# One 512-column matmul for the high and low activations in the feed-forward and MLP input projections

## The reference

```python
def conv_gated_ffn(h, w_in, conv_w, conv_b, w_out):          # D_FF = 2816, twice
    S = h.shape[1]
    g, u = jnp.split(h @ w_in, 2, axis=-1)
    gp = jnp.pad(g, ((0, 0), (CONV_WIDTH - 1, 0), (0, 0)))
    g = conv_b + sum(conv_w[k] * gp[:, k:k + S] for k in range(CONV_WIDTH))
    return (jax.nn.gelu(g) * u) @ w_out
...
f = jnp.square(jax.nn.relu(h @ w_up[i])) @ w_down[i]         # D_FF_2 = 4096, once
```

## Time and profile before

| what | value |
|---|---|
| times of the runs shown | 1197.8, 1200.43, 1200.58 us (median 1200.43) |
| span of the profiled execution, first to last instruction | 1195.7 us |
| time of the profiled execution | not listed apart; the lowest time shown is 2.1 us above the span, the median 4.7 us |
| PE busy / PEld busy | 1142.0 us (96%) / 1031.0 us (86%) |
| VectorE busy | 770.8 us (64%) |
| ScalarE busy | 631.6 us (53%) |
| mean granted TensorE clock | 0.988 of full |
| chain that ended last, by engine | PE 85%, DVE 8%, ACT 5%, issue 2% |

### The profile page before, as it was taken

How to read it: one execution, slowest core, us unless ns; L and a number is a source line. 1 busy time by engine, 2 the same in 40 slices (tenths; PEclk the granted TensorE clock), 3 DMA queues, 4 the chain that set the end, 5 groups by cost and what they waited for, 6 DMA issues and landing times.

```text
span 1195.7 us, 20980 instructions
## 1 busy us (share of the span) xinstructions
PE 1142.0 (96%) x7452; PEld 1031.0 (86%) x7452; DVE 770.8 (64%) x1132; ACT 631.6 (53%) x1084; POOL 77.5 (6%) x94
## 2 busy tenths in 40 slices
PE   7999999999999999999999999999789899999997
PEld 7977999999787998779999998998677688999996
DVE  6647766666644456877666666688977556555553
ACT  6546444444654946666444445465337646444442
POOL 0040000000100002210000000000401100000000
PEclk9999999999999999999999999899899999999999
DMA  8244455555355454443555554345000263555540
GB/s 335 74 165 158 167 189 183 191 183 189 124 187 189 154 197 161 157 160 138 179 192 178 190 180 153 99 160 181 4 4 33 88 200 119 190 184 187 188 145 35
DMA packets 51089, 185.03 MB, mean 155 GB/s; under 512 B 5696, under 2 KB 6208, under 8 KB 51040
## 3 DMA queue, kind: packets, MB, share of 16 engines
q1 hardware_dynamic: 48960, 178.28, 44.9%
q0 software_dynamic: 1504, 5.44, 1.3%
q10 hardware_dynamic: 576, 0.64, 0.2%
HBM read 183.28 MB, written 1.05 MB: 154 GB/s over the span
## 4 chain that ended last, share of the span: by engine, by line
PE 85%; DVE 8%; ACT 5%; issue 2%; DMA 0%; DVEq 0%; SPq 0%; ACTq 0%
PE ps L212 26%; PE ps L172 17%; PE ps L174 17%; PE ps L173 17%; PE ps L523 2%; ACT arena L259 2%; DVE arena L1300 2%; DVE w_lo L155 2%; PE ps L550 1%; PE ps L233 1%; PE ps L536 1%; DVE x L352 1%; PE ps L1182 1%; ACT arena L574 1%; PE ps L241 1%
## 5 line engine op out<-in xcount | busy, mean ns | idle before, releaser
L155 DVE TENSOR_TENSOR w_lo<-raw,w_hi 128x1024 fp32r<-128x1024 f32 x336 | 416.2, 1244 | 190.2 <-ACT w_hi L150 190.1
L150 ACT ACTIVATE w_hi<-raw 128x1024 fp32r<-128x1024 f32 x336 | 352.3, 1054 | 129.5 <-PE ps L212 68.8
L172 PE MATMUL ps<-a_hi,w_hi 128*128 128x256 f32 x1408 | 401.3, 285 | 2.3 <-ACT arena L815 1.4
L173 PE MATMUL ps<-a_lo,w_hi 128*128 128x256 f32 x1408 | 399.0, 283 | 0.0
L174 PE MATMUL ps<-a_hi,w_lo 128*128 128x256 f32 x1408 | 399.0, 283 | 0.0
L172 PEld LDWEIGHTS ps<-a_hi,w_hi 128*128 128x128 f32 x1408 | 270.5, 192 | 7.2 <-issue 2.7
L173 PEld LDWEIGHTS ps<-a_lo,w_hi 128*128 128x128 f32 x1408 | 270.5, 192 | 2.7
L174 PEld LDWEIGHTS ps<-a_hi,w_lo 128*128 128x128 f32 x1408 | 270.4, 192 | 0.0
L212 PE MATMUL ps<-w_hi,a_hi 128*128 128x512 f32 x496 | 158.2, 400 | 8.0 <-DVE a_lo L932 2.2
L212 PE MATMUL ps<-w_lo,a_hi 128*128 128x512 f32 x496 | 153.6, 391 | 0.0
L212 PE MATMUL ps<-w_hi,a_lo 128*128 128x512 f32 x496 | 153.4, 391 | 0.0
(11 more groups left out here) (160 smaller groups left out, 1097.8 us busy)
## 6 DMA issues: line engine op xcount, KB each, us to landing
raw<-in_w SPq DMA_DIRECT2D x336, 512.0 KB, 3.3
row<-in_rows POOLq DMA_DIRECT2D x7, 512.0 KB, 4.0
x<-in_x SPq DMA_DIRECT2D x2, 512.0 KB, 4.6
out<-x SPq DMA_DIRECT2D x2, 512.0 KB, 2.7
misc<-in_misc POOLq DMA_DIRECT2D x1, 512.0 KB, 7.5
arena<-in_ws POOLq DMA_DIRECT2D x1, 512.0 KB, 9.7
tab<-in_tables POOLq DMA_DIRECT2D x1, 320.0 KB, 3.2
tab<-in_tables POOLq DMA_DIRECT2D x1, 256.0 KB, 4.1
```

The source lines that it names most:

```text
L150: act.activation(w_hi[:, s, :], raw[:, s, :], ACT.Copy).then_inc(hi_done, 1)
L155: dve.tensor_tensor(w_lo[:, s, :], raw[:, s, :], w_hi[:, s, :].bitcast(F32), ALU.subtract).then_inc(lo_done, 1)
L172: pe.matmul(o, l_hi, r_hi, start=first, stop=False)
L173: pe.matmul(o, l_hi, r_lo, start=False, stop=False)
```

## The change

`a_hi` and `a_lo` become the two halves of one tensor `a_both`. A new function, `both_halves`, takes the place of `features` in the feed-forward and MLP input projections. For each of the 8 tiles it issues two matmuls: w_hi against both halves at once (512 columns, filling a whole PSUM bank), and w_lo against `a_hi` (256 columns) into the first half of the bank. The sum high x high + low x high stands in the first half, high x low in the second, and they have to be added afterwards. For that ScalarE copies the second half to SBUF, where it copied g before (or took the relu), and in the feed-forward it copies u's second half as well. VectorE then adds the first half from PSUM: into `pad` for g, into `F_UP` for u, into `M_RL` in the MLP. Product and square then read SBUF alone, and relu is taken in the instruction that squares. The attention, gating and mixer input projections keep `features`.

```diff
@@ -101,8 +92,8 @@
     x = sb("x", [P, TT, D])
 
 
-    a_hi = sb("a_hi", [P, 2 * KT, SEQ], F32R)
-    a_lo = sb("a_lo", [P, 2 * KT, SEQ], F32R)
+    a_both = sb("a_both", [P, 2, 2 * KT, SEQ], F32R)
+    a_hi, a_lo = a_both[:, 0, :, :], a_both[:, 1, :, :]
     cols = sb("cols", [P, COLS])
     misc = sb("misc", [P, MISC])
     tab = sb("tab", [P, TABLES])
@@ -184,6 +175,19 @@
             c = slice(k * P, (k + 1) * P)
             mm = three(pe, o, w_hi[:, s, c], w_lo[:, s, c], a_hi[:, k, :], a_lo[:, k, :],
                        k == 0, k == KT - 1)
+        mm.then_inc(unit_used, 1)
+
+    def both_halves(pe, n, bank, i=0, pre=None):
+
+        s = n % RING
+        pe.wait_ge(lo_done, n + 1 + RING * i)
+        for k in range(KT):
+            if pre is not None:
+                pe.wait_ge(pre.lo, KT * pre.n + k + 1)
+            c = slice(k * P, (k + 1) * P)
+            pe.matmul(ps[:, bank, :].rearrange("p (h t) -> p h t", h=2), w_hi[:, s, c], a_both[:, :, k, :],
+                      start=k == 0, stop=False)
+            mm = pe.matmul(ps[:, bank, 0:SEQ], w_lo[:, s, c], a_hi[:, k, :], start=False, stop=k == KT - 1)
         mm.then_inc(unit_used, 1)
 
     def tokens(pe, n, o, k0, nk, width, i=0, pre=None):
@@ -360,10 +364,11 @@
 
 
 
-    F_CV, F_GL, F_PR = cut(3072, 2, SEQ), cut(3584, 2, SEQ), cut(4096, 2, SEQ)
+    F_PT = cut(5120, 2, 2, SEQ)
+    F_CV, F_GL, F_PR, F_UP = cut(3072, 2, SEQ), cut(3584, 2, SEQ), cut(4096, 2, SEQ), cut(4608, 2, SEQ)
 
     def ffn_sems(name):
-        return signals(name, "copied conv gelu product hi lo")
+        return signals(name, "g_part u_part copied summed conv gelu product hi lo")
 
     def f_g(n0, t):
         return n0 + 3 * t - 1 if t else n0
@@ -375,9 +380,9 @@
     def ffn_in_pe(pe, f, n0, t, i=0, first=False):
         b = t % 2
         if not first:
-            pe.wait_ge(f.product, t - 1 + 2 * i)
-        features(pe, f_g(n0, t), ps[:, 4 + b, 0:SEQ], i)
-        features(pe, f_g(n0, t) + 1, ps[:, 6 + b, 0:SEQ], i)
+            pe.wait_ge(f.summed, t - 1 + 2 * i)
+        both_halves(pe, f_g(n0, t), 4 + b, i)
+        both_halves(pe, f_g(n0, t) + 1, 6 + b, i)
 
     def f_banks(t, i):
 
@@ -388,7 +393,7 @@
 
     def ffn_pe(pe, f, n0, pre):
         for n in range(2):
-            features(pe, n0 + n, ps[:, n, 0:SEQ], pre=pre)
+            both_halves(pe, n0 + n, n, pre=pre)
         ffn_in_pe(pe, f, n0, 1, first=True)
         pe.wait_ge(f.lo, 1)
         accumulate(pe, f_out(n0, 0), KT, True, False)
@@ -402,11 +407,16 @@
 
     def ffn_act_step(act, f, n0, t, i, split):
         b = t % 2
+        g_bank, u_bank = f_banks(t, i)
         act.wait_ge(unit_used, f_g(n0, t) + 1 + RING * i)
         if t >= 2:
-            act.wait_ge(f.conv, 3 * t - 3 + 6 * i)
-        act.activation(pad[:, b, 2:2 + SEQ], ps[:, f_banks(t, i)[0], 0:SEQ], ACT.Copy).then_inc(f.copied, 1)
+            act.wait_ge(f.copied, t - 1 + 2 * i)
+        act.activation(F_PT[:, b, 0, :], ps[:, g_bank, SEQ:2 * SEQ], ACT.Copy).then_inc(f.g_part, 1)
         split(0)
+        act.wait_ge(unit_used, f_g(n0, t) + 2 + RING * i)
+        if t >= 2:
+            act.wait_ge(f.summed, t - 1 + 2 * i)
+        act.activation(F_PT[:, b, 1, :], ps[:, u_bank, SEQ:2 * SEQ], ACT.Copy).then_inc(f.u_part, 1)
         act.wait_ge(f.conv, 3 * t + 3 + 6 * i)
         if t >= 2:
             act.wait_ge(f.product, t - 1 + 2 * i)
@@ -425,6 +435,10 @@
         def col(k):
             return cols[:, bass.ds(c + k + 8 * i, 1)] if not isinstance(i, int) else cols[:, c + k:c + k + 1]
 
+        g_bank, u_bank = f_banks(t, i)
+        dve.wait_ge(f.g_part, t + 1 + 2 * i)
+        dve.tensor_tensor(pad[:, b, 2:2 + SEQ], ps[:, g_bank, 0:SEQ], F_PT[:, b, 0, :],
+                          ALU.add).then_inc(f.copied, 1)
         dve.wait_ge(f.copied, t + 1 + 2 * i)
         if t >= 2:
             dve.wait_ge(f.gelu, t - 1 + 2 * i)
@@ -436,10 +450,12 @@
                                      ALU.mult, ALU.add).then_inc(f.conv, 1)
         split(0)
         split(1)
+        dve.wait_ge(f.u_part, t + 1 + 2 * i)
+        dve.tensor_tensor(F_UP[:, b, :], ps[:, u_bank, 0:SEQ], F_PT[:, b, 1, :],
+                          ALU.add).then_inc(f.summed, 1)
         dve.wait_ge(f.gelu, t + 1 + 2 * i)
-        dve.wait_ge(unit_used, f_g(n0, t) + 2 + RING * i)
-        dve.tensor_tensor(F_PR[:, b, :], F_GL[:, b, :], ps[:, f_banks(t, i)[1], 0:SEQ],
-                          ALU.mult).then_inc(f.product, 1)
+        dve.wait_ge(f.summed, t + 1 + 2 * i)
+        dve.tensor_tensor(F_PR[:, b, :], F_GL[:, b, :], F_UP[:, b, :], ALU.mult).then_inc(f.product, 1)
         dve.wait_ge(f.hi, t + 1 + 2 * i)
         dve.tensor_tensor(a_lo[:, KT + b, :], F_PR[:, b, :], a_hi[:, KT + b, :].bitcast(F32),
                           ALU.subtract).then_inc(f.lo, 1)
@@ -1431,7 +1447,12 @@
 
 
     M_PR, M_RL = cut(3072, 3, SEQ), cut(3840, 3, SEQ)
-    m_sem = signals("mlp", "relu square hi lo")
+    m_sem = signals("mlp", "part summed square hi lo")
+
+    M_PT = cut(4608, 3, SEQ)
+
+    def m_bank(t, i=0):
+        return 4 + t % 3 if t or not isinstance(i, int) else 0
 
     def m_up(t):
         return N_MLP + 2 * t - 1 if t else N_MLP
@@ -1441,11 +1462,11 @@
 
     def mlp_in_pe(pe, t, i=0):
         if t >= 3:
-            pe.wait_ge(m_sem.relu, t - 2 + 3 * i)
-        features(pe, m_up(t), ps[:, 4 + t % 3, 0:SEQ], i)
+            pe.wait_ge(m_sem.summed, t - 2 + 3 * i)
+        both_halves(pe, m_up(t), 4 + t % 3, i)
 
     def mlp_pe(pe, pre):
-        features(pe, m_up(0), ps[:, 0, 0:SEQ], pre=pre)
+        both_halves(pe, m_up(0), 0, pre=pre)
         for t in (1, 2, 3, 4):
             mlp_in_pe(pe, t)
             pe.wait_ge(m_sem.lo, t)
@@ -1462,8 +1483,8 @@
         def step(t, i, split):
             act.wait_ge(unit_used, m_up(t) + 1 + RING * i)
             if t >= 3:
-                act.wait_ge(m_sem.square, t - 2 + 3 * i)
-            act.activation(M_RL[:, t % 3, :], ps[:, 4 + t % 3 if t else 0, 0:SEQ], ACT.Relu).then_inc(m_sem.relu, 1)
+                act.wait_ge(m_sem.summed, t - 2 + 3 * i)
+            act.activation(M_PT[:, t % 3, :], ps[:, m_bank(t, i), SEQ:2 * SEQ], ACT.Copy).then_inc(m_sem.part, 1)
             split(0)
             act.wait_ge(m_sem.square, t + 1 + 3 * i)
             if t >= 3:
@@ -1474,9 +1495,12 @@
 
     def mlp_dve(dve):
         def step(t, i, split):
-            dve.wait_ge(m_sem.relu, t + 1 + 3 * i)
-            dve.tensor_tensor(M_PR[:, t % 3, :], M_RL[:, t % 3, :], M_RL[:, t % 3, :],
-                              ALU.mult).then_inc(m_sem.square, 1)
+            dve.wait_ge(m_sem.part, t + 1 + 3 * i)
+            dve.tensor_tensor(M_RL[:, t % 3, :], ps[:, m_bank(t, i), 0:SEQ], M_PT[:, t % 3, :],
+                              ALU.add).then_inc(m_sem.summed, 1)
+            dve.wait_ge(m_sem.summed, t + 1 + 3 * i)
+            dve.scalar_tensor_tensor(M_PR[:, t % 3, :], M_RL[:, t % 3, :], 0.0, M_RL[:, t % 3, :],
+                                     ALU.max, ALU.mult).then_inc(m_sem.square, 1)
             split(0)
             dve.wait_ge(m_sem.hi, t + 1 + 3 * i)
             dve.tensor_tensor(a_lo[:, KT + t % 3, :], M_PR[:, t % 3, :], a_hi[:, KT + t % 3, :].bitcast(F32),
```

## The result

The changed kernel takes 1206.78 us (median of 6 runs, 1202.59 to 1210.98), the kernel before 1199.12 beside it (6 runs, 1197.15 to 1201.97). The ratio is 1.0061, 95% interval 1.0037 to 1.0086: slower. The profiled executions have spans of 1203.1 and 1195.7 us.

What follows compares the result with a forecast made beforehand. PE was taken to bound both loops, with VectorE and ScalarE becoming the feed-forward's bound after the change. 2 x (2.5 + 1.9) - 2.8 = +6.0 us on 1200.4 gave 1206.4 us, range 1197 to 1213.

Steps and rivals of the forecast that it cites:

- forecast case: Whole kernel: VectorE's longer feed-forward step and a clock drop slow it, +6.0 us, 1203 to 1210; chance 0.48.
- VectorE's cycle: Feed-forward loop: VectorE's step becomes 0.71 + 6.24 + 0.45 + 1.15 = 8.55 us, above PE's new 8.33.
- The late low part: End of each feed-forward layer: step 21's low part, for which the last output unit waits, comes 2.5 us later.
- The clock: Last feed-forward output unit: after about 5.7 us idle, PE starts at half clock, losing 1.9 us per layer.
- the cases 1.4 and 2.4: Last output unit's loss in us: 1.4 if full clock returns 3 us after restart, 2.4 if not before the end.
- the loop shows 8.33 and PE never waits: Feed-forward loop: a sign that would show the forecast wrong, with PE's new 8.33 us step setting the pace.
- All 30 steps from t = 2 on gain 0.093 us, sum -2.8 us.: MLP loop: merged matmuls shorten each step from t = 2 on by 0.093 us, 2.8 us in all.
- one start costs 0.011 us beside its columns: PE: price of one matmul start, read from 512 columns at 0.229 us and 256 at 0.120.
- Rival 1: Feed-forward: register work runs ahead during the g addition, cycle 8.28 us, kernel faster at 1193.8 to 1197.6; chance 0.18.
- Rival 2: Last output unit: cycle is 8.55 us but the clock stays up, +2.2 us, 1202.6; chance 0.14.
- Rival 3: Feed-forward: ScalarE's extra copy or the loop's way back makes the cycle 8.70 us, 1212.4; chance 0.14.
- Rival 4: Merged matmul costs the 0.24 us of two; MLP gains nothing, feed-forward as forecast, 1209.2; chance 0.06.

Runs made afterwards that it cites:

- warm22: The changed kernel with 22 small matmuls on PE ahead of its wait for the last low part; ratio to the kernel before 1.0041.
- split_mm: The changed kernel with the 512-column matmul issued as two of 256 columns, other engines' work unchanged; span 1207.3 us.
- mlp_only: The change in the MLP alone, both feed-forwards as in the kernel before; span 1196.2 us.
- gelu_first: The changed kernel with VectorE's long-satisfied wait for gelu moved ahead of the g addition; span 1205.8 us.
- early_u: The changed kernel with VectorE's u addition moved between its first and second weight half; 1194.28 us, ratio to the kernel before 0.9966.

## Why the prediction was right

- **Direction and size.** Forecast +6.0 us, measured +7.66 between the medians and +7.4 between the spans; forecast case, inside its own 1203 to 1210. That the time itself, 1206.78, lies 0.4 us from 1206.4 is luck: the MLP gained 2.3 us less than forecast, and the kernel before took 1199.12 beside it and not 1200.4.
- **VectorE's cycle.** Forecast 8.55 us, measured 8.54 (8.61 and 8.47). Its terms: addition to tap 0.71, measured 0.76 and 0.70; last half to addition 1.15, measured 1.14; u addition to product 0.45, measured 0.52 (243.92 to 244.44), a gap of 0.10 where I took 0.04. The second weight half made that up: it follows the first after 1.52 us (241.26 to 242.78), where the two kinds of step before had 1.60 and 1.65 (248.21 to 249.86). Two small errors cancelled, which is luck. The product took 0.43 us with both operands in SBUF against 0.41 with one in PSUM (L458, 425 ns, against 414), so moving it off PSUM saved nothing.
- **The late low part.** Forecast 2.5 us per layer, 1.5 from the two unrolled steps and 1.0 from the loop. Counted from the first marker, step 1's low part starts at 29.67 us where it was 28.18 (+1.49), and step 21's at 200.67 where it was 198.12 (+2.55). With the clock kept up (warm22) the layers are 204.30 and 201.82, 2.57 and 2.49 above before.
- **The clock.** Idle time forecast 5.7 us, measured 5.37. The loss was forecast as 1.9 per layer, from the cases 1.4 and 2.4; it was 1.27 and 2.44, each just outside, and that their mean is 1.9 is luck of when the clock came back.
- **Where PE waits.** The forecast had PE idle at `f.lo` "in the later steps" and named as a sign of being wrong that "the loop shows 8.33 and PE never waits". The loop came near that sign and the forecast still held: PE kept 8.39 us and lost 0.4 us in three steps, because the low part was ready 2.9 us ahead when the loop began, a term that the prediction doesn't have. The sum doesn't need it, since the layer's end hangs on the last low part alone; but the sign was badly chosen. The wait ahead of the last unit is what decides.
- **The MLP, mis-sized.** "All 30 steps from t = 2 on gain 0.093 us, sum -2.8 us." The stage gained 0.54. The step gained 0.03 and not 0.093, 0.9 us in 30 steps. The step that failed is "one start costs 0.011 us beside its columns": I had read it as the difference of two kinds of unit (0.229 for 512 columns where the weight moves, 0.120 for 256 where the tokens move), and such a difference of near numbers carries the whole error of both. The pair measured 0.3515 to 0.3535 us, so merging saves 0.0065 to 0.0085. In the MLP half of that is lost again because the output unit takes 2.78 us instead of 2.75 (the earlier trace rows against the chain after). It does so in every kernel with merged MLP units and not in split_mm; why, the runs leave open.
- **0.35 us that aren't the MLP's.** From the first input unit to the first output unit the MLP takes 6.29 us in both kernels (1006.25 to 1012.54 before, 1014.54 to 1020.83 after), so giving units 0 and 1 nothing was about right. The 0.35 us that are missing from the 0.9 are lost before the first input unit, in the update's norm, where VectorE follows ScalarE later. First before, then after:

```profile
1002.48 0.17 DVE L272 TENSOR_SCALAR st<-st 128x2 f32<-128x2 f32 x1 [1.34 <-ACT arena L259]
```

```profile
1010.77 0.17 DVE L276 TENSOR_SCALAR st<-st 128x2 f32<-128x2 f32 x1 [1.69 <-ACT arena L263]
```

The idle time is 1.69 us in the seven kernels with the new feed-forward functions and 1.33 in mlp_only, whose MLP is the changed kernel's. So it comes with the changed feed-forward code and not with the MLP's; how, the runs leave open.

- **The total.** The feed-forward was untouched by the error in the price of a start, since PE didn't bind it: the layers' sum was forecast +8.8 and measured +8.77, and the whole miss of the total in the spans (7.4 against 6.0) is the MLP's 2.3 less the mixer's 0.5 and 0.3 us at the start.
- **Rivals.** Rival 1 (faster, the tap right behind the addition) needed a gap of 0.08 us; the timeline shows 0.28 and 0.35. Rival 2 (clock stays up, +2.2) is what warm22 built: +3.1 between the medians. Rival 3 (a step of 8.70) falls with the measured 8.54. Rival 4 (no saving at all) was nearly right for the MLP.
- **The Trainium skill's rule for a start** ("TensorE: Matmul & The Clock Gate", "Back-to-back issue gap") is 2.5 ns beside the columns, from which the prediction worked out 0.6 us for the MLP. The trace doesn't agree: merging saved 6.5 to 8.5 ns, between the Trainium skill's 2.5 and my 11. That the MLP's 0.54 us lies near 0.6 is chance, since the output unit and the norm took back a part of the saving.

## What to carry to other kernels

When work moves from the busiest engine to a less busy one, write down that engine's step as a chain of starts, with the waits inside it, and compare the sum with the period. A busy share of 64% doesn't tell it: here 1.11 us of 8.50 were free. Then look in that chain for idle time that a wait leaves in the middle, since an independent instruction costs only what is longer than that idle time there, and its full length behind it (0.11 and 0.19 us against 0.52 here); moving one addition by one place turned +0.6% into -0.3%. And where the engine that sets the pace changes, the former one gets a long wait at the end of the stage: price what its clock does there.

## What the runs showed of the hardware

- PE was idle for 5.4 us ahead of the last units and came out of it at half clock, which lasted about 3 us into one unit and through all 5.5 us of the other. Behind 4.13 us (gelu_first) the last unit was at half clock too, 5.37 us long; behind 3.57 us (split_mm) its first matmuls ran at full clock and its last at half (0.50 from 310 to 311), 4.55 us in all. With 1.49 us idle (early_u) it stayed at full clock.
- A satisfied wait with a computed value, between an instruction and a dependent one, cost 0.09 us on VectorE; ahead of both it cost nothing.
- A product of two float32 128 x 128 operands left two records and took 0.221 us at full clock.
- Merging two 256-column matmuls into one of 512 saved 6.5 to 8.5 ns, with the two column blocks 16 KB apart or side by side.
